# A later start for GpSimd's weight sums in the seven-product runs of a two-block transformer kernel

## The reference, cut to what matters

```python
def sqrelu_mlp(h, w1, w2):
    a = jnp.square(jax.nn.relu(h @ w1))
    return a @ w2
```

## Time and profile before

| | |
|---|---|
| median of 3 runs | 2265.95 us (2263.82 to 2269.12) |
| the profiled execution | 2269.03 us, of it 2267.3 us span |
| mean granted TensorE clock | 0.998 |
| sums by GpSimd in the runs | 40 pairs x 4 |
| HBM traffic | 94 GB/s over the span |

### The profile page before, as it was taken

The page is one execution under the profiler, slowest core; times in us unless marked ns, Lnnn a source line. Parts: engine busy times, 40 slices in busy tenths (PEclk is TensorE's granted clock), DMA queues, the critical chain, the costliest instruction groups (busy, mean ns, idle before and its releaser), DMA issues.

```text
span 2267.3 us, 31754 instructions
## 1 busy us (share of the span) xinstructions
PE 2217.1 (98%) x12018; PEld 1910.6 (84%) x12018; DVE 1669.3 (74%) x2601; ACT 1075.1 (47%) x1714; POOL 459.1 (20%) x330
## 2 busy tenths in 40 slices
PE   6999999999999999999999999999999999999999
PEld 4898789889788888889987788888888888888889
DVE  8965677857888886877657858884455667787787
ACT  4333444444477745444446736653344443444443
POOL 7402113313400040313330000002001004041334
PEclk9999999999999999999999999999999999999999
DMA  5483323233222223233232232124332222323323
GB/s 190 96 212 130 93 93 103 84 112 103 88 74 67 66 77 100 76 111 103 84 113 83 84 93 63 59 74 140 93 94 91 65 84 93 96 90 94 112 76 112
DMA packets 80166, 219.35 MB, mean 97 GB/s; under 512 B 18593, under 2 KB 28065, under 8 KB 79521
## 3 DMA queue, kind: packets, MB, share of 16 engines
q1 hardware_dynamic: 73568, 212.11, 30.7%
q10 hardware_dynamic: 6464, 5.47, 0.8%
HBM read 206.93 MB, written 6.29 MB: 94 GB/s over the span
## 4 chain that ended last, share of the span: by engine, by line
PE 63%; DVE 6%; ACT 2%; issue 2%; POOL 0%; DVEq 0%; ACTq 0%; POOLq 0%
PE lin L625 16%; PE lin L627 15%; PE lin L626 15%; PE tr L812 2%; PE tr L813 2%; PE tr L814 2%; PE sc L812 1%; PE sc L813 1%; PE sc L814 1%; PE tr L899 1%; DVE w_lo L1751 1%; DVE resid L1775 1%; PE sc L1069 1%; ACT w_hi L1212 0%; DVE hid_lo1a L2078 0%
## 5 line engine op out<-in xcount | busy, mean ns | idle before, releaser
L625 PE MATMUL lin<-x_hi,w_hi 128*128 128x512 f32 x1472 | 580.8, 395 | 3.8 <-DVE w_lo L1807 2.1
L627 PE MATMUL lin<-x_hi,w_lo 128*128 128x512 f32 x1472 | 573.3, 389 | 0.0
L626 PE MATMUL lin<-x_lo,w_hi 128*128 128x512 f32 x1472 | 573.1, 389 | 0.0
L1236 ACT ACTIVATE w_hi<-w_raw 128x1024 fp32r<-128x1024 f32 x253 | 268.1, 1059 | 555.5 <-PE lin L627 540.6
L1807 DVE TENSOR_TENSOR w_lo<-w_raw,w_hi 128x1024 fp32r<-128x1024 f32 x253 | 328.5, 1298 | 94.8 <-ACT w_hi L1236 92.8
L625 PEld LDWEIGHTS lin<-x_hi,w_hi 128*128 128x128 f32 x1472 | 276.4, 188 | 66.7 <-DVE w_lo L1807 4.1
L627 PEld LDWEIGHTS lin<-x_hi,w_lo 128*128 128x128 f32 x1472 | 276.3, 188 | 58.4
L626 PEld LDWEIGHTS lin<-x_lo,w_hi 128*128 128x128 f32 x1472 | 276.5, 188 | 56.6 <-issue 1.2
L1212 ACT ACTIVATE w_hi<-w_raw 128x512 fp32r<-128x512 f32 (+1 forms) x231 | 148.9, 647 | 240.7 <-POOL w_raw L2685 74.5
L1751 DVE TENSOR_TENSOR w_lo<-w_raw,w_hi 128x512 fp32r<-128x512 f32 (+1 forms) x231 | 238.1, 1031 | 5.9 <-ACT w_hi L1212 5.7
L812 PE MATMUL tr<-hid_hi,w_hi 128*128 128x256 f32 x560 | 160.1, 286 | 9.2 <-DVE resid L1775 8.1
(11 more groups left out here) (520 smaller groups left out, 4553.4 us busy)
## 6 DMA issues: line engine op xcount, KB each, us to landing
w_raw<-w SPq DMA_DIRECT2D x353, 512.0 KB, 3.5
w_raw<-w_mem SPq DMA_DIRECT2D x16, 512.0 KB, 4.4
ssm_mt<-ssm_kp SPq DMA_DIRECT2D x64, 64.0 KB, 2.8
ssm_u<-x_a SPq DMA_DIRECT2D x1, 2048.0 KB, 10.6
kv_scratch<-mem_stage SPq DMA_DIRECT2D x8, 256.0 KB, 4.8
z_b<-z_scratch SPq DMA_DIRECT2D x4, 512.0 KB, 4.6
resid<-x_b SPq DMA_DIRECT2D x1, 2048.0 KB, 11.7
out<-resid SPq DMA_DIRECT2D x8, 256.0 KB, 3.5
```

The source lines that it names most:

```text
L625: nc.tensor.matmul(out, wh[:, w], xh[:, k, 0:cols], start=(k == 0), stop=False)
L626: nc.tensor.matmul(out, wh[:, w], xl[:, k, 0:cols], start=False, stop=False)
L627: last = nc.tensor.matmul(out, wl[:, w], xh[:, k, 0:cols], start=False, stop=(k == KC - 1))
L1236: nc.scalar.activation(WH[:, b, :], raw[:, r, :], ACT.Copy).then_inc(s_hi, 1)
```

## The change

One wait is added. Sum 1 of a pair that is not the first of its run waits, beyond what it waited for, until the third product of the current pair is done.

```diff
                     if p:
                         pool.wait_ge(s_flo, f0 - PRODS + 4)
+                        pool.wait_ge(s_prod, r.prods + PRODS * (p - 1) + 3)
                     n0 = r.sums + 4 * p
```

## The result

The changed kernel is slower: ratio 1.0069 of its time to the time before (95% interval 1.005 to 1.0089), 2282.53 us median against 2271.47 for the kernel before over all runs that stood beside it; the profiled execution spans 2280.7 us. Forecast were 13.0 us more, 1.0058, which is 2279.0 us. The ratio is not that of the two medians: an execution with a mean granted clock of 0.996 or less takes mostly 7 to 10 us longer than one with 0.997 or more, whatever the kernel, and a median or a ratio depends on how many of them it holds (one of the changed kernel's six, six of the ten of experiment 6, four of the 21 timed beside that); the changed kernel's other five average 2282.2 us and the lower three of the six before 2266.3, which is 15.9 more.

What follows compares the result with a forecast made beforehand. The prediction took TensorE, busy 98% of the span, to bound the kernel. Terms of 8.9, 1.2 and 2.9 us sum to 13.0 more, on the median 2265.95 giving 2279.0 us, range 2269 to 2284.

Steps and rivals of the forecast that it cites:

- The steady pair's walk: In 15 pairs, moved sums block `lo` 6 and `lo` 7, so product 3' waits for add 1': 0.59 us a pair, 8.9.
- the weight loads: Raw slabs are released 0.8 us later, but loads land 3.5 us after issue and are needed 10 us later: hidden.
- I take 0.05, between the ends: At sum 1's added wait, GpSimd was taken to see product 3 0.05 us after VectorE, between 0 and 0.1.
- 17 pairs outside the first two of long runs: 15 steady pairs at 0.59 us and the first pair of two light runs at 0.62: 8.9 and 1.2 us lost.
- 14 first pairs: First two pairs of seven long runs: product 5 loses its wait, product 6 starts 0.21 later; 2.9 us lost.
- the bounds of the sum: Total loss over all touched pairs, with GpSimd's latency at 0 or 0.1 us: 11.4 and 14.5 us.
- A costlier block: Each new block costs a whole `lo` behind the sum, 3.9 us more over 15 pairs, 2283; chance 0.12.
- The delay is swallowed: `lo` 3' beats sum 4 to the port, so 17 pairs cost nothing and 2.9 us remain: 2269; chance 0.09.
- Faster: L2065 and L2078 get in before sum 2, relieving VectorE's backlog in long runs' first two pairs: 2256; chance 0.08.

Runs made afterwards that it cites:

- experiment 6: Kernel before plus the added wait only in the first two pairs of the seven long runs (14 of 31 pairs): run time 428.6 (+4.2), ratio 1.0046.
- experiment 5: Kernel before plus the added wait only in the 17 pairs outside the first two of long runs: run time 435.7 (+11.3), ratio 1.007.
- experiment 9: Changed kernel with sum 1 waiting for VectorE's add 3 instead of product 3: run time 433.8, +9.5 against the kernel before, ratio 1.0047.
- experiment 1: Changed kernel with the added wait at the second product instead of the third: run time 424.6, +0.3 against the kernel before, ratio 0.999.
- experiment 2: Changed kernel with the added wait at the fourth product instead of the third: run time 446.1, +21.8 against the kernel before, ratio 1.0088.
- experiment 3: Changed kernel, wait kept, with sums 1 and 2 made over only 8 of 512 columns: run time 404.9 against 424.3 before, ratio 0.9914.
- experiment 8: Kernel before with VectorE's leftover work moved to the last pair in six long runs, plus the added wait: run time 428.1, ratio 1.0028.
- experiment 4: Kernel before, without the added wait, with sums 1 and 2 made over only 8 of 512 columns: run time 404.6 against 424.3, ratio 0.9909.
- experiment 7: Kernel before, no added wait, with VectorE's leftover work moved to the last pair in six long runs: run time 409.7, -14.6, ratio 0.9933.

## Why the prediction was right in kind and short in size

**Right:** the sign, the place and the chain. The steady pair's walk came out step by step: `lo` 6 and `lo` 7 blocked, the pause ahead of add 5 gone, sums 3 and 4 and `lo` 3' late in the same order, product 3' waiting for add 1'. The blocked `lo`s end 0.54 to 0.56 behind a sum, as taken from the earlier trace rows. In the long runs' first pairs product 5 no longer waits, L2065 and L2078 run into sum 2, and product 6 starts 0.33 later than before. Hidden as forecast were the weight loads; sum 1 waits for a DMA only in the nine first pairs, as before.

**Short by 3.2 us**, 13.0 against 16.2 in the runs. The step that was mis-sized is the first of the walk, "No row shows GpSimd waiting for TensorE ... I take 0.05, between the ends": GpSimd starts **0.14** behind VectorE's view of product 3 (964.12 to 964.26), outside the ends of 0 and 0.1 that I had set. I took the upper end as a round figure and the middle as my value, though the nearest rows had already given 0.07, a difference of two other latencies; no row of before shows this one. In the changed kernel it is 0.135 to 0.137 in all 31 pairs. By the prediction's own slope (each 0.1 of latency is 0.1 in every pair) the terms become 15 x 0.68 + 2 x 0.71 + 14 x 0.30 = 15.8, so that the latency makes 2.8 of the 3.2 us:

| term | forecast | with 0.14 | measured |
|---|---|---|---|
| 17 pairs outside the first two of long runs | 10.1 | 11.6 | 11.3 (experiment 5) |
| 14 first pairs | 2.9 | 4.2 | 4.2 (experiment 6) |
| all | 13.0 | 15.8 | 16.2 (change), 15.6 (5 and 6) |

So the bounds of the sum (11.4 to 14.5) were too narrow at the top: 31 pairs multiply a small latency. The last 0.4 is a balance of small terms: 0.3 more in `mlp3.down1`, 0.6 less in the swallowed pair below, and by difference some 0.02 more in each pair, which was not traced. One reading is off by a hundredth: the first matmul behind a wait, which the prediction gives as 0.36, stands in the earlier trace rows as 0.35.

**The rivals.** *A costlier block* did not come: `lo` 6 ends 0.54 and `lo` 7 0.56 behind its sum. The rule of the Trainium skill that was weighed, "SBUF — State Buffer", section "Who interferes with whom", agrees in kind with the rows shown here (whichever comes second waits, turned round in experiment 9); the reading of it that was weighed, a whole 0.68 after the sum, does not (0.54 to 0.56). *The delay is swallowed*: this happened in one pair of the 31, the second of `mlp2.down2`, where sum 4 came 0.98 instead of 0.69 behind sum 3 and `lo` 3' was first:

```profile
1134.79 0.68 DVE L1751 TENSOR_TENSOR w_lo<-w_raw,w_hi 128x512 fp32r<-128x512 f32 x1
```

```profile
1134.97 1.65 POOL L2689 TENSOR_TENSOR w_raw<-w_raw 128x512 f32<-128x512 f32 x1 [0.98 <-DVE w_lo L1751]
```

The next product 3 did not wait, which is the 0.6 us by which this light run is shorter than the other (42.0 to 42.6). So in this pair the price of that rival was right, and the lead of 0.11 us held in the other pairs. It is not chance of one execution: a sum 4 that comes 0.98 behind sum 3 stands once in `mlp2.down2` in the profiles of experiments 1, 2, 3, 5, 8 and 9 too, and in that of the kernel before nowhere in the runs. Why GpSimd is 0.29 late there, and at sum 3 of `mlp3.down1`, is open. *Faster* did not come either: L2065 ran 1.50 us, behind sum 2, as walked.

## What to carry to other kernels

Sums on GpSimd and VectorE operations with two SBUF operands take turns, so a GpSimd operation belongs where VectorE pauses or works from PSUM, and to find that place one walks VectorE's queue operation by operation; a start 0.45 us later than the change's cost less (experiment 9) and one 1.4 us later more (experiment 2). If VectorE has work that nobody waits for, move it out of the stretch in which GpSimd works, rather than GpSimd's work into another stretch. A latency that is paid in every pair needs its bound from the same engine, and a generous one.

## What the runs showed that was not expected

GpSimd sees a product 0.14 us later than VectorE and ScalarE do (964.26 against 964.12), the same in all 31 pairs. The two sums that look free in the kernel before cost it 19.7 us in the runs together with VectorE's leftover work (experiment 4; experiment 7 wins 14.6 by moving that work), all of it at the beginning of the long runs. A small sum of 8 columns takes 0.20 us, but 0.67 when it meets a `lo`. The stretch ahead of the first run takes 334.4 to 344.2 us in eleven profiles, and most of this goes with TensorE's granted clock: in the two profiles with 344.1 and 344.2 (experiments 4 and 8) the lower level, 1.2 instead of 2.4 GHz, is granted for 20.5 us, from 142.0 and 141.5 us on, and TensorE had waited 0.88 and 0.95 us for VectorE 2 to 3 us ahead of that; in the other nine it is granted for 3.4 to 10.2 us in all, between 43 and 79 us. Why it is granted there was not looked into.
